# End of the scan: the chunk state's decay on ScalarE, y copied by two engines, the bias added to V on POOL, and the last heads handled by quarters

## The reference, cut to what matters

```python
def step(state, inp):
    r_t, w_t, k_t, v_t, a_t, b_t = inp
    sa = jnp.einsum('bhvk,bhk->bhv', state, a_t)
    state = (state * w_t[:, :, None, :]
             + sa[..., None] * b_t[:, :, None, :]
             + v_t[..., None] * k_t[:, :, None, :])
    y_t = jnp.einsum('bhvk,bhk->bhv', state, r_t)
    return state, y_t
...
mean = jnp.mean(y, axis=-1, keepdims=True)
var = jnp.mean(jnp.square(y - mean), axis=-1, keepdims=True)
y = ((y - mean) * lax.rsqrt(var + LNX_EPS)).reshape(B, S, D)
y = y * lnx_w.astype(jnp.float32) + lnx_b.astype(jnp.float32)
bonus = jnp.sum(r_h * k_h * r_k.astype(jnp.float32), axis=-1, keepdims=True) * v_h
y = y + bonus.reshape(B, S, D)
return (y * g.astype(jnp.float32)).astype(h.dtype) @ w_o
```

## Time and profile before

| | |
|---|---|
| time, median of 3 runs | 1505.71 us (1504.1 to 1505.91) |
| the profiled execution, its own time | 1502.43 us |
| its span, first to last instruction | 1500.6 us |
| mean granted TensorE clock | 0.975 |
| PE busy | 1407.9 us (94%) |
| DVE busy | 902.5 us (60%) |
| ACT busy | 721.2 us (48%) |
| POOL busy | 135.1 us (9%) |

### The profile page before, as it was taken

How to read it: one execution, slowest core, us unless ns; L and a number is a source line. 1 busy time by engine, 2 the same in 40 slices (tenths; PEclk the granted TensorE clock), 3 DMA queues, 4 the chain that set the end, 5 groups by cost and what they waited for, 6 DMA issues and landing times.

```text
span 1500.6 us, 25827 instructions
## 1 busy us (share of the span) xinstructions
PE 1407.9 (94%) x10598; PEld 1201.0 (80%) x10598; DVE 902.5 (60%) x1258; ACT 721.2 (48%) x976; POOL 135.1 (9%) x136
## 2 busy tenths in 40 slices
PE   8988999998999999997899988899999988799998
PEld 8966988987987999885576766699997765599997
DVE  5565655566576645566976686555456665355553
ACT  5454545446544544454464233354354655254452
POOL 0162011100000100100100011000000123000000
PEclk9998999999999999999999999999999999899999
DMA  8733465564655566553653000455574631255462
GB/s 293 241 89 125 151 206 176 170 192 154 217 165 171 164 216 198 193 171 93 188 148 114 4 4 2 155 182 181 159 241 141 217 101 56 71 172 184 157 218 85
DMA packets 86429, 231.29 MB, mean 154 GB/s; under 512 B 15860, under 2 KB 21636, under 8 KB 86312
## 3 DMA queue, kind: packets, MB, share of 16 engines
q1 hardware_dynamic: 85752, 227.53, 47.7%
q0 software_dynamic: 560, 2.11, 0.4%
HBM read 228.53 MB, written 1.08 MB: 153 GB/s over the span
## 4 chain that ended last, share of the span: by engine, by line
PE 82%; DVE 8%; ACT 4%; issue 2%; POOL 2%; DMA 2%; SPq 0%; DVEq 0%; ACTq 0%; POOLq 0%
PE PS L429 50%; PE PS L432 29%; PE PS L444 3%; ACT SH L401 1%; POOL AB L790 1%; DVE SL L404 1%; DVE SL L407 1%; DVE AB L764 1%; ACT AB L774 0%; POOL SM L858 0%; DMA ST<-in_w_attn_in 0%; DMA ST<-in_rw_w_r 0%; DMA ST<-in_rw_w_k 0%; DVE LG L1644 0%; DMA ST<-in_w_conv_in 0%
## 5 line engine op out<-in xcount | busy, mean ns | idle before, releaser
L407 DVE SCALAR_TENSOR_TENSOR SL<-ST,SM,SH 128x1024 fp32r<-128x1024 f32 (+1 forms) x256 | 314.6, 1249 | 176.3 <-ACT SH L401 137.2
L401 ACT ACTIVATE SH<-ST,SM 128x1024 fp32r<-128x1024 f32 (+1 forms) x256 | 282.5, 1122 | 213.9 <-PE PS L432 141.8
L429 PE MATMUL PS<-XH,SH 128*128 128x256 f32 x1224 | 344.3, 281 | 1.8 <-DVE XL L578 1.8
L432 PE MATMUL PS<-XH,SL 128*128 128x256 f32 x1224 | 344.5, 281 | 0.0
L429 PE MATMUL PS<-XL,SH 128*128 128x256 f32 x1224 | 343.5, 281 | 0.0
L404 DVE TENSOR_TENSOR SL<-ST,SH 128x1024 fp32r<-128x1024 f32 (+1 forms) x161 | 205.3, 1291 | 158.0 <-ACT SH L401 138.1
L429 PE MATMUL PS<-SH,XH 128*128 128x512 f32 x576 | 241.5, 419 | 35.2 <-DVE XL L1845 8.3
L401 ACT ACTIVATE SH<-ST 128x1024 fp32r<-128x1024 f32 (+1 forms) x161 | 166.6, 1051 | 159.0 <-PE PS L432 133.3
L432 PE MATMUL PS<-SH,XL 128*128 128x512 f32 x576 | 233.9, 406 | 0.0
L429 PEld LDWEIGHTS PS<-XH,SH 128*128 128x128 f32 x1224 | 231.4, 189 | 3.1 <-ACT SH L401 1.9
L429 PE MATMUL PS<-SL,XH 128*128 128x512 f32 x576 | 233.6, 406 | 0.0
(11 more groups left out here) (305 smaller groups left out, 1412.4 us busy)
## 6 DMA issues: line engine op xcount, KB each, us to landing
ST<-in_ffn_w_gu SPq DMA_DIRECT2D x80, 512.0 KB, 4.9
ST<-in_w_mlp_up SPq DMA_DIRECT2D x64, 512.0 KB, 4.7
ST<-in_w_mlp_down SPq DMA_DIRECT2D x64, 512.0 KB, 4.4
ST<-in_ffn_w_down SPq DMA_DIRECT2D x44, 512.0 KB, 4.3
ST<-in_w_attn_in SPq DMA_DIRECT2D x24, 512.0 KB, 5.1
ST<-in_w_conv_in SPq DMA_DIRECT2D x24, 512.0 KB, 4.5
ST<-in_w_ple_gate SPq DMA_DIRECT2D x16, 512.0 KB, 4.3
ST<-in_kv_w SPq DMA_DIRECT2D x16, 512.0 KB, 4.3
```

The lines of the kernel that those rows point to most:

```text
L401: a = ac.do(lambda e: e.activation(h[p0:p1, 0:cols], t[p0:p1, 0:cols], ACT.Copy, scale=sc), ready, t_gt, pe_done.get(i - NSPLIT))
L407: b = ve.do(lambda e: e.scalar_tensor_tensor(l[p0:p1, 0:cols], t[p0:p1, 0:cols], sc, h[p0:p1, 0:cols].bitcast(F32), ALU.mult, ALU.subtract ...
L429: pe.go(lambda e: e.matmul(o, l, r, start=start, stop=stop, skip_group_check=skip))
L432: return pe.do(lambda e: e.matmul(o, l, r, start=start, stop=stop, skip_group_check=skip))
```

## The change: what it does

Six edits in one stretch of the program:

- In `tail`, the scaling by the decay for g = 0 and 1 is an activation on ScalarE with a scale; VectorE keeps the spreading. For g = 2, where TC is not needed, one VectorE operation scales and spreads.
- y of half c = 1 is copied by VectorE, of half c = 0 by ScalarE.
- The bonus on POOL waits for the last matmul that reads V (`v_read`) and not for y, and POOL adds the bias to it. The bias addition on VectorE is gone.
- `block_split` serves the first eight heads only. For the last eight, `quarter(d)` transposes four heads for both m and splits them.
- `finish(2)` and `finish(3)` run together for their first five steps (up to the power) and then one after the other, with units 0 to 2 and the first quarter between.
- The last four units: m = 0 with units 4 and 5, then the quarter of d = 3, then units 6 and 7, then m = 1 with all four.

```diff
+        v_read.append(t)   # in post: the last matmul that reads V
...
+            if g < 2:
+                tc_ = ac.do(lambda e, g=g, o=o, dec=dec: e.activation(z.TC[:, g, :], o, ACT.Copy, scale=dec), tf, t_pe)
+                tb2 = ve.do(lambda e, g=g, tb_=tb_: e.tensor_tensor(tb_, z.TC[:, g, :].unsqueeze(1).to_broadcast([128, 2, 64]), bd2, ALU.mult), tc_)
+            else:
+                tb2 = ve.do(lambda e, tb_=tb_, o=o, dec=dec: e.scalar_tensor_tensor(tb_, o.unsqueeze(1).to_broadcast([128, 2, 64]), dec, bd2, ALU.mult, ALU.mult), tf, t_pe)
...
+            if c:
+                y = ve.do(lambda e, c=c, src=src: e.tensor_copy(Ra[hf(c), :, pc], src), t)
+            else:
+                y = ac.do(lambda e, c=c, src=src: e.activation(Ra[hf(c), :, pc], src, ACT.Copy), t)
...
-        bv = po.do(lambda e: e.tensor_tensor(cols(VN), cols(VN), b64(bo), ALU.mult), toks, t_bo)
+        bv = po.do(lambda e: e.tensor_tensor(cols(VN), cols(VN), b64(bo), ALU.mult), v_read[2 * d:2 * d + 2], t_bo)
+        bv = po.do(lambda e: e.tensor_tensor(VN[:, :, 256 * d:256 * d + 256], VN[:, :, 256 * d:256 * d + 256], row(lb), ALU.add), bv, lbt)
...
-        c = ve.do(lambda e: e.tensor_tensor(y2, y2, row(lb), ALU.add), c, lbt)
-        yield
...
+    def quarter(d):
+
+        b, bs = d, slice(2 * d, 2 * d + 2)
+        wait_banks([b])
+        pe.wait(y_res[d])
+        for m in range(2):
+            for k in range(2):
+                t = tr_t(bank(b, m * 256 + k * 128, m * 256 + k * 128 + 128), Ra[:, m, d * 256 + k * 128:d * 256 + k * 128 + 128])
...
+        h = ac.do(lambda e: e.activation(h_, ps, ACT.Copy), t, scan_done)
+        l = ve.do(lambda e: e.tensor_tensor(l_, ps, h_.bitcast(F32), ALU.subtract), h, scan_done)
...
-    res = [block_split(m, 0, m) for m in range(2)]
-    run([finish(d, y_tok[2 * d:2 * d + 2]) for d in (2, 3)])
+    res = [block_split(m) for m in range(2)]
+    last = {d: finish(d, y_tok[2 * d:2 * d + 2]) for d in (2, 3)}
+    for _ in range(5):
+        for d in (2, 3):
+            next(last[d])
     wait_banks([4, 5, 6, 7])
     pe.wait(res)
-    kind_a(XS[0], range(4), (4, 5, 6, 7), last=False)
-    res = [block_split(m, 1, 2 + m) for m in range(2)]
+    kind_a(XS[0], range(1), (4, 5, 6, 7), last=False)
+    run([last[2]])
+    kind_a(XS[0], range(1, 3), (4, 5, 6, 7), first=False, last=False)
+    res = [quarter(2)]
+    run([last[3]])
...
+    kind_a(XS[0], range(3, 4), (4, 5, 6, 7), first=False, last=False)
+    us = take_group(4)
+    t = [None, None]
+    for m in range(2):
+        for j, (i, h, l) in enumerate(us):
+            if m == 0 and j % 2 == 0:
+                if j:
+                    res.append(quarter(3))
+                pe.wait(res)
+            pe.wait(split_tok[i])
+            for n in range(2):
+                t[m] = mm3(bank(4 + 2 * m + n), [x[:, 4 + j, m * 128:(m + 1) * 128] for x in XS[0]], [x[:, n * 512:(n + 1) * 512] for x in (h, l)], False, j == 3)
+            if m:
+                pe_done[i] = t[1]
...
-    pe.wait(res)
-    t = kind_a(XS[0], range(4, 8), (4, 5, 6, 7), first=False, end=True)
```

More of the change, by code:

```diff
@@ L1593, in emit @@
         lanes.append(z)
-    y_tok = []
+    y_tok, v_read = [], []
     def two(z, lo, n):
@@ L1757, in tail @@
                 tf = mm_t(o, z.ET[:, m, c, :], z.TC[:, g - 1, :], False, True)
-            tc_ = ve.do(lambda e, g=g, o=o: e.tensor_scalar(z.TC[:, g, :], o, small(384 + 8 * g + p), None, ALU.mult), tf, t_pe)
-            tb2 = ve.do(lambda e, g=g: e.tensor_tensor(z.TB[:, g, :].rearrange("p (h v) -> p h v", h=2),
-                                                       z.TC[:, g, :].unsqueeze(1).to_broadcast([128, 2, 64]), bd2, ALU.mult), tc_)
+            dec = small(384 + 8 * g + p)
+            tb_ = z.TB[:, g, :].rearrange("p (h v) -> p h v", h=2)
+            if g < 2:
[3 more added lines that the diff above has]
+                tb2 = ve.do(lambda e, tb_=tb_, o=o, dec=dec: e.scalar_tensor_tensor(tb_, o.unsqueeze(1).to_broadcast([128, 2, 64]), dec, bd2, ALU.mult, ALU.mult), tf, t_pe)
             yield
@@ L1766, in tail @@
         for c in range(2):
-            y = ac.do(lambda e, c=c: e.activation(Ra[hf(c), :, pc], bank(z.bk[c], 0, 256, 64 * c, 64 * c + 64).rearrange("p (m t) -> p m t", m=2), ACT.Copy), t)
+            src = bank(z.bk[c], 0, 256, 64 * c, 64 * c + 64).rearrange("p (m t) -> p m t", m=2)
+            if c:
+                y = ve.do(lambda e, c=c, src=src: e.tensor_copy(Ra[hf(c), :, pc], src), t)
+            else:
+                y = ac.do(lambda e, c=c, src=src: e.activation(Ra[hf(c), :, pc], src, ACT.Copy), t)
             bfree[z.bk[c]] = y
@@ L1788, in emit @@
     lb, lbt, lbi = param()
-    y_res = [[], []]
+    y_res = {}
     def finish(d, toks):
@@ L1825, in finish @@
         yield
-        c = ve.do(lambda e: e.tensor_tensor(y2, y2, row(lb), ALU.add), c, lbt)
-        yield
         c = ve.do(lambda e: e.tensor_tensor(y2, y2, VN[:, :, 256 * d:256 * d + 256], ALU.add), c, bv)
         yield
-        y_res[d // 2].append(ve.do(lambda e: e.tensor_tensor(y2, y2, GG[:, :, 256 * d:256 * d + 256], ALU.mult), c, tgg))
+        y_res[d] = (ve.do(lambda e: e.tensor_tensor(y2, y2, GG[:, :, 256 * d:256 * d + 256], ALU.mult), c, tgg))
     run([lane(k, lanes[k]) for k in range(4)])
@@ L1834, in emit, with block_split @@
     scan_done = [[z.fr, z.tail_free] for z in lanes] + [y_tok]
[L1836 to L1840, removed]
+    def block_split(m):
+        cs, bs = slice(m * 128, m * 128 + 128), slice(0, 4)
+        wait_banks([m])
+        pe.wait(y_res[0], y_res[1])
         for k in range(4):
-            t = tr_t(bank(b, k * 128, k * 128 + 128), Ra[:, m, n * 512 + k * 128:n * 512 + k * 128 + 128])
-        ps = bank(b).rearrange("p (b t) -> p b t", b=4)
+            t = tr_t(bank(m, k * 128, k * 128 + 128), Ra[:, m, k * 128:k * 128 + 128])
+        ps = bank(m).rearrange("p (b t) -> p b t", b=4)
@@ L1844, in block_split @@
         h = ac.do(lambda e: e.activation(XS[0][0][:, bs, cs], ps, ACT.Copy), t, scan_done)
         l = ve.do(lambda e: e.tensor_tensor(XS[0][1][:, bs, cs], ps, XS[0][0][:, bs, cs].bitcast(F32), ALU.subtract), h, scan_done)
+        bfree[m] = l
+        return [h, l]
+    def quarter(d):
[5 more added lines that the diff above has]
+                t = tr_t(bank(b, m * 256 + k * 128, m * 256 + k * 128 + 128), Ra[:, m, d * 256 + k * 128:d * 256 + k * 128 + 128])
+        ps = bank(b).rearrange("p (m b t) -> p b m t", m=2, b=2)
+        h_, l_ = [x[:, bs, :].rearrange("p b (m t) -> p b m t", m=2) for x in XS[0]]
+        h = ac.do(lambda e: e.activation(h_, ps, ACT.Copy), t, scan_done)
+        l = ve.do(lambda e: e.tensor_tensor(l_, ps, h_.bitcast(F32), ALU.subtract), h, scan_done)
@@ L1846, in block_split @@
         bfree[b] = l
         return [h, l]
-    res = [block_split(m, 0, m) for m in range(2)]
-    run([finish(d, y_tok[2 * d:2 * d + 2]) for d in (2, 3)])
-    par_done(lwi, y_res)
-    par_done(lbi, y_res)
+    res = [block_split(m) for m in range(2)]
[3 more added lines that the diff above has]
+            next(last[d])
     wait_banks([4, 5, 6, 7])
     pe.wait(res)
-    kind_a(XS[0], range(4), (4, 5, 6, 7), last=False)
@@ L1856, in emit @@
-    res = [block_split(m, 1, 2 + m) for m in range(2)]
+    kind_a(XS[0], range(1), (4, 5, 6, 7), last=False)
[3 more added lines that the diff above has]
+    run([last[3]])
+    par_done(lwi, list(y_res.values()))
+    par_done(lbi, list(y_res.values()))
+    kind_a(XS[0], range(3, 4), (4, 5, 6, 7), first=False, last=False)
[12 more added lines that the diff above has]
+                pe_done[i] = t[1]
@@ L1878, in plain_chain @@
         add_plain((4, 5, 6, 7), t, m)
-    hr_free[0] = [scan_done, t[1], q, y_res]
+    hr_free[0] = [scan_done, t[1], q, list(y_res.values())]
     hx_free[0] = hx_free[1] = hr_free[0]
```

## The result

The changed kernel takes 1495.72 us (median of 11 executions, 1489.28 to 1504.45) beside 1504.41 for the kernel before (11, 1502.85 to 1508.83): ratio 0.994, 95% interval 0.9921 to 0.9958. It is faster, by 8.7 us. The prediction was 1498.3 and a gain of 7.4; of the 2.6 between 1498.3 and 1495.72, 1.3 is that the kernel before had a median of 1504.41 this time and not 1505.71, and 1.3 is a larger gain.

A forecast was written before the change was run, and what follows sets the result against it. The prediction took ScalarE at the output projection's entrance and VectorE in its middle as the limits. Terms 0.4 + 2.74 + 5.45 - 1.2 = 7.4 us gave 1498.3 from a median of 1505.71, range 1495.1 to 1502.6.

The forecast's parts named there:

- start of the last 36: Output projection: TensorE starts its last 36 matmuls at 939.8, not 942.54, following VectorE's forecast operation list: 2.74 us gained.
- 36 and not 48 behind it: Output projection after the second stop: 36 matmuls take 8.3 us against 13.77 for 48, gaining 5.45.
- clock after the stops: Output projection: charge of 1.2 us for TensorE's clock falling after its two stops, bounds 0 and 2.7.
- sum in S: Terms 2.74, 5.45 and -1.2 within S, from first transposition after the second tail to first transposition of x.
- The side sentence: If the clock falls after the first stop: units 0-2 1.5 us later, quarters about 0.75, second stop below 2.
- 0.4 up to the tail's end: Scan through second tail: gain 0.2 us from y copies plus 0.2 from removed bias additions; bounds 0 and 1.5.
- The 0.2 of the bias additions in the scan: Second run's scan: VectorE loses two adds (1.29 us), of which 0.2 was counted as gain; bounds 0 and 1.29.
- POOL's exclusion: Rival, chance 0.13: in the tails POOL and VectorE exclude each other, costing 0.6 us a tail; gain 6.2, time 1499.5.
- Longer TB products beside POOL: Sign of being wrong: in the tail, VectorE's TB products take longer than before, or come late, beside POOL; no size.
- VectorE as late as today: Rival, chance 0.11: output projection's last XL subtraction still comes at 941.1; gain only 3.2 us, time 1502.5.
- given back: Rival, chance 0.08: the next stage starts 7 us earlier but waits for its weights; time 1505.7.
- slower: Rival, chance 0.04: clock stays at 1.2 GHz throughout the output projection, ending 8.4 us later; time 1513.7.

The follow-up runs named there:

- run again: The changed kernel measured again, nothing edited: 1497.09 us (6 executions) beside 1505.35 for the kernel before, ratio 0.9937.
- profile after: Profiled execution of the changed kernel in its first measurement, nothing further edited, the slowest of eleven: 1504.45 us.
- bias on VectorE: The changed kernel with the bias added by VectorE again, POOL keeping the bonus: stretch from second tail's end to first transposition of x 30.27 us; no median.
- quarters alone: Against the kernel before: only the new output projection by quarters, with old tail and normalisation; 1500.53 us (6 executions), ratio 0.9965.
- all of y on ScalarE: The changed kernel with all eight y copies on ScalarE again: 1498.18 us in one execution.
- the scan's part alone: Against the kernel before: only decay on ScalarE, y by two engines and bias on POOL, with the old output projection; 1499.90 us (5 executions), ratio 0.9965.
- late bonus: The changed kernel with POOL's bonus and bias operations waiting for y again, after the tail: stretch from second tail's end to first transposition of x 29.83 us; no median.
- the other order: The changed kernel with second quarter after unit 4 and splits of units 6, 7 and two ffn units after heads 3: 1495.66 us, ratio 0.9944.
- again2: The changed kernel measured once more, nothing edited: 1496.37 us (8 executions) beside 1504.71 for the kernel before, ratio 0.9953.

## Why the prediction was right

The stretch and the two limits in it were the right ones. Term by term, with P and S of the run again (clock held) and of the profile after (clock fell):

| term | forecast | measured, clock held | clock fell |
|---|---|---|---|
| start of the last 36 | 2.74 | 23.41 - 20.43 = 2.98 | 23.41 - 21.17 = 2.24 |
| 36 and not 48 behind it | 5.45 | 13.77 - 8.43 = 5.34 | 13.77 - 8.44 = 5.33 |
| clock after the stops | -1.2 | 0 | 0, it is in the first row |
| sum in S | 7.0 | 8.32 | 7.57 |

- **The term that was mis-sized is the clock's charge of 1.2.** It came from a stop of 2.54 after which the clock fell. The second stop was forecast at 2.4; it was 2.05 or 1.50 in the changed kernel and 1.50 to 2.17 in the other runs with quarters that still have it, and the clock never fell behind it. After the first, 2.01, it fell in three executions and held in five (below). The side sentence, that a fall there makes the quarters 0.75 later and the second stop shorter, came out in the end: the last XL starts 0.74 later from the tail's end (20.34 against 19.60), the stop is 1.50 and S 0.75 longer. But TensorE transposes the quarters 1.3 later, and the 0.75 was put down without a working; that it fits to the hundredth is luck.
- **2.74 was 2.98, by the list that was forecast.** From the tail's end to VectorE's multiplication by the inverse deviation it was to take 8.75 and took 8.77 in the run again, to the last XL 19.87 and 19.60. Of the 2.98, 1.60 is ScalarE's four copies, as forecast. The other 1.14, forecast from the new list as a whole, the runs take apart: the two bias additions are worth 1.44 (bias on VectorE), and the new order by itself brings nothing at this point (quarters alone: 23.46 against 23.41). They add up: 20.43 + 1.60 + 1.44 = 23.47, beside the 23.46 of the quarters alone.
- **5.45 was 5.34**, and its two halves were right: 12 matmuls of 0.231 are 2.8, the clock's fall behind the second stop 2.6.
- **0.4 up to the tail's end** was of the right size with other parts. The products of the second run start 3.64 after its first transposition (866.58 to 870.22) against 3.78 before (860.88 to 864.66), 0.14 where 0.2 was forecast. The two tails are 0.12 shorter each, which I had at nothing. The 0.2 of the bias additions in the scan is too small to be seen beside TensorE's idle time without a releaser (below) and stays unshown.
- **POOL's exclusion** (rival, 0.13) is real in its mechanism and empty in its price: 0.65 on a product, nothing on TensorE, whose tail is 6.84 with and without it. Longer TB products beside POOL were listed as a sign of being wrong; they were seen, and the sign was too strict.
- **VectorE as late as today, given back, slower:** VectorE is not as late (P above). The next stage begins with the same one wait of 1.1 us for VectorE, before and after, and with none for a load; the time is kept. The clock was at 0.50 for 3.4 us of S in the profile after, and for at most 6.8 in the runs (all of y on ScalarE, the scan's part alone).

## What to carry to other kernels

Where an engine stands still twice in a stretch, ask of each stop whose list ends last, and count an operation on that list at the distance from start to start that it has there (0.73 in a chain, 0.60 where two chains alternate); here one list (VectorE's) gives P of the runs with the bias on VectorE, with the late bonus and with the quarters alone from that of the run again to 0.06 us. Bringing independent matmuls ahead of a wait paid twice, by their own time and by the clock that a shorter stop kept. Work moved to POOL should lie beside VectorE work with slack: the same two operations delayed nobody under the tail, and behind it VectorE's list by 0.9.

## What the runs showed that I had not expected

- **The same stop, two answers of the clock.** After the first stop of 2.01 the granted clock fell to the 1.2 GHz level in three profiled executions (the profile after, the late bonus, the bias on VectorE) and held in five (again twice, the scan's part alone, the other order twice); after 2.15 it held once. What decides it stays open. With stops of 3.61 to 4.74 in S the clock always fell (five), with second stops of 1.50 to 2.17 never (nine).
- **TensorE idles in the scan for nothing that the trace shows.** The waits of TensorE from the first lanes to the second tail's end, in the profile after and in again2 (engine, what it waits for, us, times, longest; "issue" is idle time for which the profile shows no releaser):

```profile
PE PS L429 <- issue: 7.2, 9, 1.4
...
PE PS L432 <- issue: 1.2, 1, 1.2
```

```profile
PE PS L429 <- issue: 3.4, 5, 1.0
```

8.4 us in an execution of 1504.45, 3.4 in one of 1493.54, of the same program; 4.4 in the kernel before. The spans of these two differ by 10.9: the lanes start 3.56 apart, from there to the tail's end they differ by 3.38, in S by 0.76 and behind S by 3.2. The clock counts against the idle time here: over these runs of lanes its mean was 0.99 and 0.92, and TensorE was busy for 98.90 and 102.79. So the idle time is one part of the spread of 15 us between executions; the clock, and the code ahead of the lanes and behind S, which the change does not touch, are others. What TensorE waits for stays open; no run here separates it.
